# A first up projection in seven block products in place of eight, for 26 of its 32 panels

## What is computed

```python
x = layer_norm(DEEPNORM_ALPHA * x + mix, ln1_g[l], ln1_b[l])
h = jnp.square(jax.nn.relu(jnp.einsum("bsd,df->bsf", x, w_ff1[l])))
ff = jnp.einsum("bsf,fd->bsd", h, w_ff2[l])
x = layer_norm(DEEPNORM_ALPHA * x + ff, ln2_g[l], ln2_b[l])
```

## Time and profile before

| | us |
|---|---|
| runs (3): lowest, median, highest | 1443.78, 1444.7, 1444.82 |
| the profiled execution, its time | 1445.06 |
| its span (first to last instruction) | 1442.8 |
| busy in the span: TensorE | 1418.2 |
| busy in the span: VectorE | 817.0 |
| busy in the span: ScalarE | 612.7 |
| busy in the span: GpSimd | 124.9 |

### The profile page before, as it was taken

The page is one execution under the profiler, slowest core; times in us unless marked ns, Lnnn a source line. Parts: engine busy times, 40 slices in busy tenths (PEclk is TensorE's granted clock), DMA queues, the critical chain, the costliest instruction groups (busy, mean ns, idle before and its releaser), DMA issues.

```text
span 1442.8 us, 20161 instructions
## 1 busy us (share of the span) xinstructions
PE 1418.2 (98%) x7966; PEld 1136.9 (79%) x7966; DVE 817.0 (57%) x1408; ACT 612.7 (42%) x1113; POOL 124.9 (9%) x119
## 2 busy tenths in 40 slices
...
DMA packets 41501, 130.94 MB, mean 91 GB/s; under 512 B 4928, under 2 KB 7360, under 8 KB 41408
## 3 DMA queue, kind: packets, MB, share of 16 engines
...
q10 hardware_dynamic: 864, 1.05, 0.2%
...
## 4 chain that ended last, share of the span: by engine, by line
PE 93%; DVE 3%; ACT 2%; issue 1%; DMA 1%; POOL 0%; SPq 0%; POOLq 0%; DVEq 0%; ACTq 0%
PE bank L1306 90%; PE bank L1309 3%; ACT Fm L1703 1%; DVE Fm L2061 1%; DVE Fm L2166 1%; DMA Fm<-in_x_dram 0%; DMA Fm<-in_relb_dram 0%; SPq L2762 0%; POOL Fm L2665 0%; DVE Fm L2065 0%; ACT Whi L1703 0%; POOL Xf L2665 0%; DVE sm L2065 0%; ACT Rm L1703 0%; DVE Fm L2069 0%
## 5 line engine op out<-in xcount | busy, mean ns | idle before, releaser
L1306 PE MATMUL bank<-Rm,Whi 128*128 128x512 f32 (+1 forms) x2840 | 874.5, 389 | 9.3 <-ACT Whi L1703 6.0
L1306 PEld LDWEIGHTS bank<-Rm,Whi 128*128 128x128 f32 x2840 | 532.8, 188 | 120.7 <-ACT Whi L1703 6.0
L1306 PE MATMUL bank<-Rm,Wlo 128*128 128x512 f32 (+1 forms) x1420 | 565.4, 398 | 2.0 <-issue 1.8
L2061 DVE TENSOR_TENSOR Wlo<-Wraw,Whi 128x1024 fp32r<-128x1024 f32 (+2 forms) x225 | 283.8, 1265 | 112.5 <-ACT Whi L1703 111.8
L1306 PEld LDWEIGHTS bank<-Rm,Wlo 128*128 128x128 f32 x1420 | 267.6, 188 | 61.4 <-issue 7.5
L1703 ACT ACTIVATE Whi<-Wraw 128x1024 fp32r<-128x1024 f32 (+2 forms) x225 | 232.5, 1038 | 187.1 <-PE bank L1306 181.3
L1306 PE MATMUL bank<-Xr,Whi 128*128 128x512 f32 (+1 forms) x760 | 228.4, 382 | 0.0
L2665 POOL TENSOR_TENSOR Fm<-Fm 128x512 f32<-128x512 f32 (+1 forms) x89 | 102.4, 1157 | 780.0 <-ACT Fm L1703 489.2
L1703 ACT ACTIVATE Fm<-bank 128x512 f32<-128x512 f32 (+4 forms) x200 | 92.4, 482 | 170.7 <-PE bank L1306 106.0
L1306 PEld LDWEIGHTS bank<-Xr,Whi 128*128 128x128 f32 x760 | 141.1, 188 | 27.9
L1306 PE MATMUL bank<-Xr,Wlo 128*128 128x512 f32 (+1 forms) x380 | 145.6, 383 | 0.0
...
## 6 DMA issues: line engine op xcount, KB each, us to landing
...
```

The costliest lines, as they stand in the source:

```text
L1306: return e.matmul(o, l, r, start=first, stop=last)
L2061: return e.tensor_tensor(o, x, y, op)
```

## The change

Up panels 5 to 30 are taken in 13 pairs. A pair's product is a 2 x 2 block matrix (two panels by two halves of the input features) times a 2 x 2 block matrix (two halves of the input features by two halves of the tokens, `EARLIER` and `LATER`, 256 each). Before, it was eight block products (2 x 2 x 2). Now it is seven, with sums of blocks as operands. Each block product is 4 steps of three matmuls with 256 columns, 12 matmuls in all. Their order on TensorE is 1, 5, 2, 6, 3, 4, 7 (`PRODUCTS`), and they use three banks: "total" (1, 6, 7), "single" (2, 4) and "fifth" (5, 3).

- Sums of y's blocks are made once, by GpSimd: four operations of 256 columns for each of four q, 16 in all. ScalarE rounds them (8 instructions of 512 columns), VectorE subtracts for their low parts (8 of 512).
- Sums of the weights' blocks are made for each pair by VectorE, from the raw panels: "blocks" 0 and 1, two operations of 512 columns each. "blocksplit" (ScalarE, 1024 columns) and "blocklow" (VectorE, 1024 columns) make their two parts, each twice a pair. Half 0 feeds products 5 and 6, half 1 products 3 and 7. The pair's second panel needs only its second half split and lowered (512 columns).
- The results are put together outside TensorE: ScalarE copies the bank after products 1, 5, 6 and 4 (256 columns each) into the ReLU tiles, VectorE adds the bank after products 2 and 3 (256 columns) and 7 (512 columns). Product 6 waits for the copy after product 1, product 3 for that after 5, product 7 for that after 6, product 4 for the addition after 2.
- ReLU then works in place in SBUF, and the square moves from VectorE to ScalarE, for all 32 up panels; the low part of the hidden tile becomes an item of its own, "hidlow".
- In `project`, the block sums of the next pair are made in the last two panels ahead of it, after the pending lows. Between pairs, `seven_up` places them.
- From the fourth up panel on the ring "P" has six banks, (3, 7, 1, 2, 4, 0). The load of the constants `gdnconsts`, and the reuse of a `Wraw` slot of a pair, get one more wait each. `finished(n)` takes the place of the wait for a panel's count.

The diff, cut to its core:

```diff
+PAIRS = [n for n, (_, i) in enumerate(PANELS) if doubled(n) and i % 2 == 1]
+PAIR_NO = {n: r for r, n in enumerate(PAIRS)}
+def pair_of(n):
+    return n - 1 + PANELS[n][1] % 2 if doubled(n) else None
+PRODUCTS = (1, 5, 2, 6, 3, 4, 7)
+def product_end(n, p):
+    return 7 * PAIR_NO[n] + PRODUCTS.index(p) + 1
+
...
+    def blocks_of(n, half):
+        do("blocks", n, half)
+        do("blocksplit", n, half)
+        do("blocklow", n, half)
 
...
                 low_weights()
+                if n + 2 in PAIRS:
+                    blocks_of(n + 2, 0)
+                if n + 1 in PAIRS:
+                    blocks_of(n + 1, 1)
...
+    def seven_up(i, before):
+        n = st["taken"]
+        assert PANELS[n] == ("w_ff1", i) and n in PAIRS
+        ready_weights(n + 2)
+        low_weights(n + 2)
+        st["taken"] += 2
+        follows = n + 2 in PAIRS
+        for bank in ("total", "single", "fifth"):
+            do(bank, n)
+        do("product", n, 1)
+        do("copy", n, 1)
+        do("product", n, 5)
+        do("copy", n, 5)
+        before()
+        ready_weights(n + 3)
+        do("product", n, 2)
+        do("addup", n, 2)
+        low_weights(n + 3)
+        do("product", n, 6)
+        do("copy", n, 6)
+        ready_weights(n + 4)
+        if follows:
+            do("blocks", n + 2, 0)
+            do("blocks", n + 2, 1)
+            do("blocksplit", n + 2, 0)
+        do("product", n, 3)
+        do("addup", n, 3)
+        low_weights(n + 4)
+        if follows:
+            do("blocklow", n + 2, 0)
+        do("relu2", i)
+        do("product", n, 4)
+        do("copy", n, 4)
+        do("product", n, 7)
+        st["done"] = n + 2
+        do("addup", n, 7)
+        do("hidlow", i)
+        if follows:
+            do("blocksplit", n + 2, 1)
+            do("blocklow", n + 2, 1)
+        do("relu2", i + 1)
 
...
     first = project_first([("w_ff1", i) for i in range(3)], apart=True)
+    do("ring", "P", (3, 7, 1, 2, 4, 0))
+    waiting = []
+    def hidden_lows():
+        while waiting:
+            do("hidlow", waiting.pop())
     for kind, i in FF1:
-        if kind == "up":
+        if kind == "up" and doubled(NTH["w_ff1", i]):
+            if NTH["w_ff1", i] in PAIRS:
+                seven_up(i, hidden_lows)
+                waiting.append(i + 1)
+                if NTH["w_ff1", i] + 2 not in PAIRS:
+                    hidden_lows()
+        elif kind == "up":
             n = first[i] if i < 3 else project("w_ff1", i)
             do("relu2", i)
+            do("hidlow", i)
+            if i == 2:
+                for q in range(4):
+                    do("ysums", q)
...
+        def stationary(n, p):
+            if p in (1, 2, 4):
+                slot, first = (n % HL, 0 if p == 1 else 512) if p < 3 else ((n + 1) % HL, 512)
+                return tuple(x[:, slot, first:first + 512] for x in (Whi, Wlo))
+            half, first = {5: (0, 0), 6: (0, 512), 3: (1, 0), 7: (1, 512)}[p]
+            return tuple(x[:, first:first + 512] for x in combined(half)[0:2])
+        def copied(n, p):
+            return SG["copied"], 4 * PAIR_NO[n] + (1, 5, 6, 4).index(p) + 1
+        def added(n, p):
+            return SG["added"], 3 * PAIR_NO[n] + (2, 3, 7).index(p) + 1
+
...
+                elif what == "product":
+                    n, p = i
+                    r = PAIR_NO[n]
+                    if p in (1, 2, 4):
+                        of = n + 1 if p == 4 else n
+                        w.wait_ge(SG["w_hi"], of + 1)
+                        w.wait_ge(*low_part(of))
+                    else:
+                        w.wait_ge(SG["block_hi"], 2 * r + (1 if p > 4 and p < 7 else 2))
+                        w.wait_ge(SG["block_lo"], 2 * r + (1 if p > 4 and p < 7 else 2))
+                    if p in (1, 2, 5):
+                        bank_free({1: "total", 2: "single", 5: "fifth"}[p], n)
+                    elif p == 4:
+                        w.wait_ge(*added(n, 2))
+                    else:
+                        w.wait_ge(*copied(n, {6: 1, 3: 5, 7: 6}[p]))
+                    o = bank({1: "total", 6: "total", 7: "total", 2: "single", 4: "single", 5: "fifth", 3: "fifth"}[p], n)
+                    o = o[:, LATER if p == 4 else EARLIER]
+                    hi, lo = stationary(n, p)
+                    for k in range(4):
+                        for part in moving_made(k, p):
+                            w.wait_ge(*part)
+                        xh, xl = moving(k, p)
+                        s = slice(128 * k, 128 * k + 128)
+                        add(o, lo[:, s], xh, p in (1, 2, 5) and k == 0)
+                        add(o, hi[:, s], xl)
+                        m = add(o, hi[:, s], xh, False, k == 3)
+                    m.then_inc(SG["product"], 1)
...
+                elif what == "blocksplit":
+                    n, half_ = i
+                    r = PAIR_NO[n]
+                    w.wait_ge(SG["blocks_p" if half_ else "blocks"], 2 * r + 2)
+                    if r > 0:
+                        w.wait_ge(SG["product"], product_end(PAIRS[r - 1], 7 if half_ else 6))
+                    hi, _, raw = combined(half_)
+                    act(hi, raw).then_inc(SG["block_hi"], 1)
+                elif what == "ysums":
+                    q, = i
+                    for n in range(2):
+                        w.wait_ge(SG["y_sums"], 4 * q + (2 if n == 0 else 4))
+                        act(y_part(q, n)[0], F(Y_SUMS + 2 * q + n)).then_inc(SG["y_sum_hi"], 1)
+                elif what == "copy":
+                    n, p = i
+                    j = PANELS[n][1] + (p in (4, 5))
+                    w.wait_ge(SG["product"], product_end(n, p))
+                    w.wait_ge(SG["squared"], j - 2)
+                    b = bank({1: "total", 6: "total", 5: "fifth", 4: "single"}[p], n)
+                    act(F(RELU + j % 3)[:, EARLIER if p in (1, 4) else LATER], b[:, LATER if p == 4 else EARLIER]).then_inc(SG["copied"], 1)
                 elif what == "relu2":
                     j, = i
-                    b = panel(NTH["w_ff1", j])
+                    n = NTH["w_ff1", j]
+                    f, g = F(RELU + j % 3), F(SQUARE + j % 3)
+                    if doubled(n):
+                        w.wait_ge(*added(pair_of(n), 3 if pair_of(n) == n else 7))
+                        act(f, f, ACT.Relu).then_inc(SG["relu"], 1)
+                    else:
+                        b = panel(n)
+                        if j >= 3:
+                            w.wait_ge(SG["squared"], j - 2)
+                        act(f, b, ACT.Relu).then_inc(SG["relu"], 1)
+                    w.wait_ge(SG["relu"], j + 1)
                     if j >= 3:
-                        w.wait_ge(SG["squared"], j - 2)
-                    act(F(RELU + j % 3), b, ACT.Relu).then_inc(SG["relu"], 1)
+                        w.wait_ge(SG["hid_lo"], j - 2)
+                    act(g, f, ACT.Square).then_inc(SG["squared"], 1)
                     w.wait_ge(SG["squared"], j + 1)
                     if j >= 9:
-                        w.wait_ge(SG["panel"], NTH["w_ff2", 8 * ((j - 9) // 8) + 7] + 1)
-                    act(R(HID[j % 9][0]), F(SQUARE + j % 3)).then_inc(SG["hid_hi"], 1)
+                        w.wait_ge(*finished(NTH["w_ff2", 8 * ((j - 9) // 8) + 7]))
+                    act(R(HID[j % 9][0]), g).then_inc(SG["hid_hi"], 1)
...
+                elif what == "blocks" and i[1] == 0:
+                    n, _ = i
+                    r = PAIR_NO[n]
+                    s1, s2 = F(BLOCKS), F(BLOCKS + 1)
+                    if r > 0:
+                        w.wait_ge(SG["block_lo"], 2 * r - 1)
+                        w.wait_ge(SG["blocks_p"], 2 * r)
+                    else:
+                        w.wait_ge(SG["y_sum_lo"], 8)
+                    w.wait_ge(*loaded(n))
+                    w.wait_ge(*loaded(n + 1))
+                    tt(s1, Wraw[:, (n + 1) % RAW, 0:512], Wraw[:, (n + 1) % RAW, 512:1024], ALU.add).then_inc(SG["blocks"], 1)
+                    w.wait_ge(SG["blocks"], 2 * r + 1)
+                    tt(s2, s1, Wraw[:, n % RAW, 0:512], ALU.subtract).then_inc(SG["blocks"], 1)
+                elif what == "blocks" and i[1] == 1:
+                    n, _ = i
+                    r = PAIR_NO[n]
+                    s2, s4, s3 = (F(BLOCKS + j) for j in (1, 2, 3))
+                    if r > 0:
+                        w.wait_ge(SG["block_lo"], 2 * r)
+                    w.wait_ge(SG["blocks"], 2 * r + 2)
+                    w.wait_ge(*loaded(n))
+                    w.wait_ge(*loaded(n + 1))
+                    tt(s3, Wraw[:, n % RAW, 0:512], Wraw[:, (n + 1) % RAW, 0:512], ALU.subtract).then_inc(SG["blocks_p"], 1)
+                    tt(s4, Wraw[:, n % RAW, 512:1024], s2, ALU.subtract).then_inc(SG["blocks_p"], 1)
+                elif what == "blocklow":
+                    n, half_ = i
+                    w.wait_ge(SG["block_hi"], 2 * PAIR_NO[n] + half_ + 1)
```

(47 more changed lines are left out.)

70 lines of the change are left out of this document (56 added, 14 removed).

## The result

The changed kernel took 1447.67 us in the median of nine runs (1446.29 to 1452.12), beside 1444.82 us for the kernel before on the same chip (nine runs, 1443.78 to 1445.27): ratio 1.0024, 95% interval 1.0016 to 1.0033. So it is slower by 0.24%, 3.5 us by the ratio and 2.9 by the medians. The execution that was profiled took 1450.89 us, with a span of 1449.1.

A forecast was written before the change was run, and what follows sets the result against it. TensorE, busy 98% of the span, was taken as the bound. Span 1442.8 + 8.4 (first group) - 5.3 (later groups) = 1445.9; a difference of +3.1 on the median 1444.7 gave 1447.8 us, range 1443.8 to 1451.5.

The forecast's parts named there:

- TensorE's price of a pair: Up projection in steady flow: 84 matmuls of 256 columns at 0.120 us, 10.08 us a pair against 10.88.
- Rival (e): Paired products: 256-column matmuls are paced by weight loads of 188 ns, +64 us; chance 0.01.
- The groups' gain: Later groups: 1.7 us in each of two groups of four, 1.9 in the last of three, together 5.3.
- The forecast loop: ScalarE and VectorE, one copy of product 4 to the next: 11.03 us a pair, against TensorE's 10.08.
- for an instruction that waits on its own engine's previous result 0.06: Helper engines: 0.06 us added for each such wait, an estimate between 0.02 and 0.10.
- Rival (c): Later groups: the helpers' loop takes 11.4 us a pair, gains fall to 3.0, 1450.1 us; chance 0.10.
- The first group's loss: First group, walked through the helpers' written order: first down panel at 452.4 against 444.04, a loss of 8.4 us.
- the port: GpSimd's sums of y lock VectorE out of SBUF: 0.4 us counted at y's low parts, bounds 0 and 2.
- Rival (b): First group: y's lows 2 us late, GpSimd's last sums late for ScalarE, +1.5 to 2.5 us, 1450; chance 0.10.
- rival (a): First group: TensorE's clock drops to 1.2 GHz around its gap, costing 2.2 us, 1450.0; chance 0.20.
- two smaller gaps precede: First group: argument against a clock drop, that two smaller TensorE gaps come before the one over 4 us.
- Rival (d): First group: ScalarE's waits for VectorE are shorter, a 4 us loss giving 1443.4 us, not slower; chance 0.18.

The follow-up runs named there:

- h: Changed kernel with pairs only from panel 9, y's sums one quarter each behind panels 3 to 6, and no square in paired panels: 1436.48 us.
- a: Changed kernel with up panels 5 to 8 taken singly, pairs only from panel 9: 1445.43 us, ratio 1.0001 to the kernel before.
- i: Changed kernel without GpSimd's sixteen sums of y, plain y tiles rounded and lowered in their place: 1448.7 us.
- g: Changed kernel with unused matmuls of y's rounded high tile filling the waits before the first pair's products 1, 5 and 6: 1448.37 us.
- b: Changed kernel with no panel taken in a pair, y's sums, roundings and low parts kept: 1449.54 us.
- d: Changed kernel with panel 4's ReLU, square and rounding behind the first pair's copies after products 1 and 5 on ScalarE: 1446.53 us.
- j: Changed kernel with pairs from panel 7 on and y's sums two quarters each behind panels 3 and 4: 1443.82 us.
- k: Changed kernel with the first pair's block roundings behind the chains of panels 3 and 4, not ahead of them: 1446.47 us.

## Why the prediction was right

1447.8 was forecast and 1447.67 measured; the direction (slower, 0.60) and the reason (the first group loses more than the groups gain) held. Two terms were mis-sized, in opposite directions.

- **TensorE's price of a pair**, 10.08 us from the 0.120 pitch: measured 10.08 in the second pair, and 40.31 for four (h). Rival (e) is out.
- **The groups' gain**, 5.3 forecast, 6.3 measured (2.2, 1.9, 2.2). The forecast loop of 11.03 us is 10.87 in ScalarE's timeline of the changed kernel, from one row of two copies to the next:

```profile
521.75 0.64 ACT L1895 ACTIVATE Fm<-bank 128x256 f32<-128x256 f32 x2
...
532.62 0.64 ACT L1895 ACTIVATE Fm<-bank 128x256 f32<-128x256 f32 x2
```

  The mis-sized term is "for an instruction that waits on its own engine's previous result 0.06". In ScalarE's timelines of the experiments a rounding begins 0.66 to 0.67 us after the square that it depends on (a: 415.85 after 415.19), whose duration is 0.63: so 0.03 to 0.04. The loop has some six such waits (four in the two chains, two in the block sums), which comes to the 0.16 that the loop is shorter. The stalls stand where it said, before product 6 in the third and fourth pairs of a group, and h shows that they are the loop's. Rival (c) is out.
- **The first group's loss**, 8.4 forecast, 10.8 measured. The walk named the right waits in the right order, and its copy "seen at 436.5", 41.5 after T0, came 42.3 after (product 6 at 436.61). The 0.8 fits the mis-sized term of the port. It was taken as 0.4 at y's own low parts, where TensorE in fact waited for nothing; the price was 1.1 us and stood at the low parts of y's sums, the walk's "VectorE's eight subtractions run behind at 0.60", which overlap GpSimd's last operations (17.13 us for sixteen, forecast 13). Without GpSimd (i) product 6 starts 1.4 us sooner. Rival (b) was thus partly right, in kind and not in place.
- **The clock.** The other 1.5 us are rival (a), given 0.20. The step that kept it out of the sum, "two smaller gaps precede", failed: the level fell within the wait of 3.4 us before product 1, and a second time behind the wait of 1.8 us before product 6, without any gap of the forecast's "over 4 us". g prices it by itself at 1.5, where the rival said 2.2; the longer, first stretch at the low level lay under the wait for the copy. It came in the profiled executions of b, d, i, j and k too, though not in a's. And not only in profiled ones: all nine executions of the changed kernel had a mean granted clock of 0.994 to 0.996, where those of the kernel before, beside the experiments, had 0.997 to 1.000. TensorE: Matmul & The Clock Gate, the Trainium skill, says in Part 1 that activity releases a clock that is low by default; after the restart at 425.26 the rows show it at 0.50 first and full from 434.6, which agrees.
- **Rival (d)**, that ScalarE's waits for VectorE are shorter than the walk: they were 4.38 and 2.49, as the walk had them (4.3 and 2.6). Rival (d) is out. Where the order is changed (k) they shrink to 2.56 and 0.87, and the loss falls to 7.2.
- **The sum.** 8.4 - 5.3 = 3.1 against 10.8 - 6.3 = 4.5 in the stage. That the median still came within 0.2 us of the forecast is partly luck: two errors of opposite sign, of 1.0 and 2.4 us, and an execution-to-execution spread of 5.8. The span of the profiled execution is 1.4 us above the forecast by its stage and another 1.8 by what lies outside, and no profile exists of an execution at the median.
